# Gate tables laid by token tile, the last tile stored in four portions, and the first four u tables fetched while the gates are still being spread

## What is computed

```python
def peer_ffn(h, w_query, sub_keys, expert_u, expert_v):
    ...
    idx = jnp.take_along_axis(cand_i, pos, axis=-1).reshape(t_count, PEER_HEADS * PEER_TOPK)
    gate = jax.nn.softmax(top_s, axis=-1).reshape(t_count, PEER_HEADS * PEER_TOPK).astype(h.dtype)
    def block(args):
        tb, ib, gb = args
        act = jax.nn.gelu(jnp.einsum('pkd,pd->pk', expert_u[ib], tb), approximate=False) * gb
        return jnp.einsum('pk,pkd->pd', act, expert_v[ib])
```

## Time and profile before

| | |
|---|---|
| median of 3 runs | 4523.65 us (4521.7 to 4831.31) |
| profiled execution, own time | 4513.02 us |
| its span | 4511.1 us |
| TensorE products busy | 3640.2 us, 81% |
| VectorE, ScalarE busy | 2232.9 us (49%), 1565.4 us (35%) |
| spreading, 512 tokens | about 969 to 1155 us of the span |
| experts, 512 tokens | about 1155 to 2117 us |
| spreading, 256 tokens | about 2481 to 2592 us |
| experts, 256 tokens | about 2592 to 3070 us |

### The profile page before, as it was taken

The page is one execution under the profiler, slowest core; times in us unless marked ns, Lnnn a source line. Parts: engine busy times, 40 slices in busy tenths (PEclk is TensorE's granted clock), DMA queues, the critical chain, the costliest instruction groups (busy, mean ns, idle before and its releaser), DMA issues. The chain is left out here.

```text
span 4511.1 us, 58281 instructions
## 1 busy us (share of the span) xinstructions
PE 3640.2 (81%) x19637; PEld 2637.3 (58%) x19637; DVE 2232.9 (49%) x4378; ACT 1565.4 (35%) x2639; POOL 168.1 (4%) x344
## 2 busy tenths in 40 slices
PE   7958987958699999998885599998367767767776
PEld 5638965547588888886555589997236322222223
DVE  5535643999566666665358778884442100000001
ACT  4424432138344444442241666663122111111111
POOL 0015600000000000000000000000000000000000
PEclk8979988979899999999897899999669788788888
DMA  4320023407654444553111599993212599999996
GB/s 181 112 78 13 14 94 121 168 26 221 223 186 176 168 174 179 186 186 131 55 47 38 150 371 312 311 310 123 112 38 85 211 428 427 428 428 427 427 428 272
DMA packets 331811, 909.62 MB, mean 202 GB/s; under 512 B 46592, under 2 KB 167168, under 8 KB 306176
## 3 DMA queue, kind: packets, MB, share of 16 engines
q1 hardware_dynamic: 331648, 907.42, 53.4%
HBM read 854.38 MB, written 52.95 MB: 201 GB/s over the span
## 5 line engine op out<-in xcount | busy, mean ns | idle before, releaser
L2002 PE MATMUL pd<-h_parts,u_parts 128*128 128x512 f32 x2048 | 472.5, 391 | 38.1 <-DVE u_parts L2088 38.1
L2015 PE MATMUL po<-act_parts,v_parts 128*128 128x512 f32 x2048 | 483.5, 393 | 9.4 <-DVE v_parts L2093 2.8
L2002 PEld LDWEIGHTS pd<-h_parts,u_parts 128*128 128x128 f32 x2048 | 386.3, 189 | 119.1 <-DVE u_parts L2088 38.3
L2015 PEld LDWEIGHTS po<-act_parts,v_parts 128*128 128x128 f32 x2048 | 383.7, 189 | 104.2 <-DVE v_parts L2093 21.2
L3126 PE MATMUL pb<-moe_ring,moe_xs 128*32 128x512 f32 x2048 | 330.7, 757 | 140.0 <-DMA moe_ring<-in_moe_gu 125.1
L3177 DVE TENSOR_TENSOR moe_hidden<-moe_silu,pg 128x512 f32<-128x512 f32 x16 | 11.0, 688 | 661.6 <-PE pg L3115 576.2
L2206 PE MATMUL pd<-h_parts,u_parts 128*128 128x256 f32 x2048 | 268.1, 284 | 38.5 <-DVE u_parts L2285 38.5
L2206 PEld LDWEIGHTS pd<-h_parts,u_parts 128*128 128x128 f32 x2048 | 264.6, 192 | 50.1 <-DVE u_parts L2285 39.1
L2216 PE MATMUL po<-v_parts,act_parts 128*128 128x512 f32 x1024 | 260.0, 398 | 0.9 <-DVE act_parts L2301 0.9
L395 PE MATMUL ps<-h_terms,w_terms 128*128 128x512 f32 x960 | 224.8, 397 | 37.6 <-DVE w_terms L408 37.6
L2052 ACT ACTIVATE acts<-pd 128x512 f32<-128x512 f32 x128 | 76.5, 598 | 492.7 <-PE pd L2002 492.7
(11 more groups left out here) (486 smaller groups left out, 5839.0 us busy)
## 6 DMA issues: line engine op xcount, KB each, us to landing
moe_ring<-in_moe_gu SPq DMA_DIRECT2D x128, 2048.0 KB, 27.0
u_stream<-in_peer_u SPq DMA_DIRECT2D x256, 512.0 KB, 6.1
v_stream<-in_peer_v SPq DMA_DIRECT2D x256, 512.0 KB, 4.3
moe_ring<-in_moe_down SPq DMA_DIRECT2D x64, 2048.0 KB, 26.3
ada_ring<-in_ada_w SPq DMA_DIRECT2D x20, 2048.0 KB, 14.2
g_stream<-peer_gates SPq DMA_DIRECT2D x128, 256.0 KB, 5.5
peer_gates<-gate_stage_even SPq DMA_DIRECT2D x3, 8192.0 KB, 30.3
peer_gates<-gate_stage_odd SPq DMA_DIRECT2D x3, 8192.0 KB, 30.3
```

The lines of the kernel that those rows point to most:

```text
L2002: m = pe.matmul(pd[:, j, 0:T], us[:, j, w, c], h[:, w, c], start=(c + w == 0), stop=(c == DC - 1 and w == 1))
L2015: m = pe.matmul(po[:, (c + b) % 4, 0:T], vs[:, j, w, (c + b) * P:(c + b) * P + P], aparts[:, 4 * half + j, w], start=(j + w == 0), stop=(j ...
```

## The change

- The sets are written out one after the other instead of in loops. On VectorE is_first now stands ahead of is_second; the product with the gate follows it.
- The gate tensor in HBM is laid out [tile, i2, i1, token of the tile]. A tile's store is 64 KB in one piece for each partition. A table's g is then read as 128 partitions x 4 (wide) or 2 (narrow) pieces of 512 B.
- The last tile's store is issued as four portions (LastTile), 32 values of i1 each, 16 KB a partition. The end of the spreading stage waits for the tiles before it, not for these. Whoever needs the gates, or writes over the odd stage, waits in the experts stage for the portions concerned.
- The indicator matrices first_ind and second_ind now lie in the four slots of the ring of u tables (u_stream). When the last but one set is multiplied, SyncE fetches u tables 0 and 1 into the two slots that it used, and after the last set tables 2 and 3.
- The buffers of the experts are laid so that the odd stage lies under those which are needed late: in the wide layer v, its parts and the activation parts, in the narrow one v0 to v3 (portion 0), half of the v parts (portion 1), u4 to u7 (portion 2), v4 to v7 (portion 3).
- In the narrow layer the first eight tables are fetched in another order.

The diff, cut to its core:

```diff
-                        dve.tensor_tensor(is_second[:, x], number4, marks(1), ALU.is_equal).then_inc(second.h, 1)
...
-                        dve.tensor_tensor(is_first[:, x], number4, marks(0), ALU.is_equal).then_inc(first.h, 1)
+                    dve.tensor_tensor(is_first[:, x], number4, marks(0, t0), ALU.is_equal).then_inc(first.h, 1)
...
+                    dve.tensor_tensor(is_second[:, x], number4, marks(1, t0), ALU.is_equal).then_inc(second.h, 1)
+                    dve.wait_ge(second.h, second.at(n + 1))
...
             @block.sync
             def _(sp):
-                for tile in range(tiles):
-                    sp.wait_ge(taken.h, taken.at(4 + (tile + 1) * TURNS * 4))
-                    sp.dma_start(gates[:, :, tile * P:tile * P + P].rearrange("i p t -> p i t"), stage[tile % 2][:]).then_inc(written[tile % 2].h, DMA_DONE)
-                for w in written:
-                    sp.wait_ge(w.h, w.at(DMA_DONE * tiles // 2))
+                for tile in range(tiles - 1):
+                    sp.wait_ge(taken.h, taken.at(2 * PER * (tile + 1)))
+                    sp.dma_start(gates[tile], stage[tile % 2][:]).then_inc(written[tile % 2].h, DMA_DONE)
+                for x in range(2):
+                    sp.wait_ge(joined.h, joined.at(2 * (ALL - 1 + x)))
+                    for j in range(2 * x, 2 * x + 2):
+                        fetch_u(k, sp, tables, u, j)
+                sp.wait_ge(taken.h, taken.at(2 * ALL))
+                last.write(sp, gates, stage[(tiles - 1) % 2])
+                for tile in range(max(0, tiles - 3), tiles - 1):
+                    sp.wait_ge(written[tile % 2].h, written[tile % 2].at(DMA_DONE * (tile // 2 + 1)))
...
+class LastTile:
+    def write(self, eng, gates, stage):
+        for n in range(self.PARTS):
+            rows = slice(n * self.ROWS, (n + 1) * self.ROWS)
+            eng.dma_start(gates[self.tile, :, rows], stage[:, rows]).then_inc(self.landed[n].h, DMA_DONE)
...
 def experts_wide(k, u, v, gates, h, acc, xT, gain, us, ub, last):
...
-                    sp.dma_start(gb[:, j], gates[bass.ds(s * 4 + j, 1)].rearrange("a p t -> (a p) t")).then_inc(g_in[j].h, DMA_DONE)
+                    sp.dma_start(gb[:, j].rearrange("p (a t) -> p a t", t=P), gates[:, :, bass.ds(s * 4 + j, 1)].rearrange("a p i t -> p a (i t)")).then_inc(g_in[j].h, DMA_DONE)
...
                 for j in range(4):
-                    get_u(0, j, True)
+                    get_u(1, j, False)
+                last.wait(sp, 0)
                 for j in range(4):
                     get_g(0, j, True)
-                for j in range(4):
-                    get_u(1, j, False)
                 period(0, True)
+                last.wait(sp, 1, 2, 3)
...
                     squash(0, j, True)
                     high_u(1, j)
+                    if j == 0:
+                        last.wait(sc, 1, 2, 3)
                     high_a(0, 0, j, True)
...
 def experts_narrow(k, u, v, gates, h, xT, gain, us, spare, u0, ident, last):
...
-                for j in range(RAW):
-                    get(0, j, True)
+                last.wait(sp, 0)
+                for j in range(HALF):
+                    get_g(0, j)
+                    get_v(0, j)
+                for j in range(HALF, RAW):
+                    get_g(0, j)
+                last.wait(sp, 1, 2)
+                for j in range(HALF, RAW):
+                    get_u(0, j)
+                last.wait(sp, 3)
+                for j in range(HALF, RAW):
+                    get_v(0, j)
...
                     squash(n, j, early)
+                    if start and j == 2:
+                        last.wait(sc, 1)
                     high_v(n, j, early)
```

More of the change, by code:

```diff
@@ L1775, in peer_select, with peer_scatter @@
         x.done(2 * DMA_DONE)
-def peer_scatter(k, selT, T, consts, gates, even, terms):
+def peer_scatter(k, selT, T, consts, gates, even, odd, tables, u, terms, last):
     nc = k.nc
@@ new lines, in take @@
+                def take(n, b):
+                    tile, at = n // PER, (n % PER) * SET + 4 * b
+                    act.wait_ge(joined.h, joined.at(2 * n + b + 1))
+                    act.activation(stage[tile % 2][:, :, at:at + 4], ps[:, 2 * (n % 2) + b, :].rearrange("p (t n) -> p n t", t=4), ACT.Copy).then_inc(taken.h, 1)
+                widen(0)
+                widen(1)
+                for n in range(ALL):
+                    tile = n // PER
+                    if n % PER == 0 and tile >= 2:
+                        act.wait_ge(written[tile % 2].h, written[tile % 2].at(DMA_DONE * (tile // 2)))
+                    take(n, 0)
+                    take(n, 1)
+                    if n + 2 < ALL:
+                        widen(n + 2)
@@ new lines, with __init__, wait, done @@
+class LastTile:
+    PARTS = 4
+    ROWS = NK // PARTS
+    def __init__(self, k, tiles):
+        self.tile = tiles - 1
+        self.landed = [k.sig(f"sc_last{n}") for n in range(self.PARTS)]
+    def write(self, eng, gates, stage):
+        for n in range(self.PARTS):
+            rows = slice(n * self.ROWS, (n + 1) * self.ROWS)
+            eng.dma_start(gates[self.tile, :, rows], stage[:, rows]).then_inc(self.landed[n].h, DMA_DONE)
+    def wait(self, eng, *parts):
+        for n in parts:
+            eng.wait_ge(self.landed[n].h, self.landed[n].at(DMA_DONE))
+    def done(self):
+        for s in self.landed:
+            s.done(DMA_DONE)
@@ L1928, in done, with experts_wide @@
         self.high.done(DC)
-def experts_wide(k, u, v, gates, h, acc, xT, gain, us):
+def experts_wide(k, u, v, gates, h, acc, xT, gain, us, ub, last):
     nc = k.nc
@@ L2153, in experts_wide, with experts_narrow @@
     added.done(N_SUPER * DC)
-def experts_narrow(k, u, v, gates, h, xT, gain, us, spare, ident):
+def experts_narrow(k, u, v, gates, h, xT, gain, us, spare, u0, ident, last):
     nc = k.nc
```

186 lines of the change are left out of this document (88 added, 98 removed).

## The result

| | before | changed |
|---|---|---|
| median of 7 runs each | 4519.28 us | 4495.99 us |
| range of them | 4510.6 to 4523.65 us, and one of 4831.31 | 4489.75 to 4501.08 us |
| ratio of the runs, 95% interval | | 0.995 (0.994 to 0.9959) |
| profiled execution, its span | 4513.02, 4511.1 us | 4501.08, 4499.3 us |

The change takes 23 us, 0.5%, which is a real gain and less than the 2% that would have counted as faster. The forecast was 22.2 us. The one run of 4831.31 us was in a slower state of the chip and isn't in the ratio.

What follows compares the result with a forecast made beforehand. Two seams of some 75 us, with only a store and a fetch at work, were taken as the gain, VectorE's spreading pace and the DMA queue as risks; 11.8 + 10.4 = 22.2 us off 4523.65 gives 4502, range 4484 to 4532.

Steps and rivals of the forecast that it cites:

- Part 1: Spreading on VectorE: the product waits for the comparison just before it, costing 0.115 us a set, 11.1 us in all.
- the 0.35 us row: VectorE's idle time after the cast of the keys, behind a dependency and a branch; the high-end price per set.
- Rival 2: Spreading: VectorE's wait costs 0.43 us a set, not 0.115; 30 us more than forecast, 4532 us; chance 0.09.
- Part 2: Gates laid by tile: 8.39 MB stored in 19.7 us in place of 28.9; smaller g reads stay hidden, cost 0.
- Rival 1: Seams: the store stays at 28.9 us, both seams end 9.2 us later than forecast; 4520 us; chance 0.13.
- Rival 4: Experts: 512 B g reads at wide pitch are slow in HBM; 4672 us; chance 0.04 full, 0.04 mild.
- The pitch effect: Experts' g reads: large row pitches slow packets to about 58 ns, a narrow table 3.5 us, still hidden, sum unchanged.
- Part 3: Wide seam: early u tables start TensorE sooner, table 4 waits behind the store; net of VectorE's cost 11.8 us gained.
- The clock's 2.9 us: Wide seam: after 7 us idle TensorE loses its clock, and 2.9 us of the gain go again.
- Part 4: Narrow seam: first second-layer product at 2594.4, then u4 late at 2602.3; net gain 10.4 us.
- Rival 3: Seams: the queue doesn't hold u4 and g0 back until all portions pass; gain some 40 us, 4484; chance 0.06.

Runs made afterwards that it cites:

- e1: Changed kernel with VectorE's old order in the spreading (is_second, is_first, product); ratio to the kernel before 0.9934.
- e7: Changed kernel with the gates in the old layout (512 B store packets) and the last tile stored by one DMA; ratio to the kernel before 0.9981.
- e4: Changed kernel with the last tile stored by one DMA instead of four portions; ratio to the kernel before 0.9963.
- e2: Changed kernel with the gates laid [i1, i2, token] as before (512 B store packets), four portions kept; ratio to the kernel before 0.9984.
- e3: Changed kernel with the last tile's four portions issued by ScalarE on its own queue; ratio to the kernel before 0.9958.
- e6: Changed kernel with the wide layer's fetches issued g0, u4, g1, u5 and so on, not u4 to u7 then g0 to g3; ratio to the kernel before 0.9934.
- e9: Changed kernel with VectorE's old order and g0, u4, g1, u5 and so on, store on SyncE's queue; median 4484.54 us, ratio to the kernel before 0.9926.
- e5: Changed kernel with u0 to u3 fetched behind the last tile's portions, not ahead of them; ratio to the kernel before 0.9972.
- e8: Changed kernel with VectorE's old order, portions on ScalarE's queue, and g and u4 to u7 issued alternately; ratio to the kernel before 0.9923.

## Why the prediction was right

**Part 1, the order on VectorE.** Right, mechanism and size. Forecast 0.115 us a set and 11.1 us, measured 0.12 and 11.4 (e1). The price was taken from a plain dependent pair elsewhere in the trace (rows at 959.73 and 960.99 in the earlier trace rows) and not from the 0.35 us row behind a branch. Rival 2 is out. The statement that the loops cost nothing was slightly wrong: the rewriting saved 2.2 us. It holds for VectorE's 2.34 us a set, but not for the first set of each further tile (2.74).

**Part 2, the gates laid by tile.** Right for the new store, too large for the difference. The estimate of 422 GB/s for large store packets, drawn from two rows for small ones, stands beside 429 measured. In part that is luck: it rests on the step from 290 GB/s at 512 B to 350 at 1 KB, and e7 shows 512 B packets at 350 too. The 9.2 us by which each store should get shorter were 7.1 in the wide layer and 4.9 in the narrow one, from issue to landing with four u tables ahead (e7 against e4). Rival 1 is out, and with it the Trainium skill's figure (DMA: Bandwidth & Descriptors, Specifications) that 512 B is enough for line rate: this chip stored at 290 GB/s, for a while at 350, with 512 B, and at 429 with 16 KB. (The two layouts also differ in where in HBM the pieces go; no run varies the size alone.) What the layout is worth is shown by two pairs: 11.4 us with a single store (e7 against e4) and 12.9 with four portions (e2 against the changed kernel), about half of the change's gain and more than any other part. The reads of 512 B cost nothing, as forecast. From the wide seam's end to the narrow spreading it is 1289.0 us against 1288.2, and in the narrow experts, from table 5 to the row with the last products with v, both layouts take 463.9 us (changed 463.90, before 463.89, e2 463.89). The rise of the DMA share from 0.48 to 0.51 is just the step that the forecast's sizes give, (0.93 - 0.69) / 7.2 = 0.03. Rival 4 is out. The pitch effect of the same page (Latency and other measured facts), which by the prediction's reckoning would have doubled these packets and made the share 0.64, doesn't appear. It isn't refuted by that: the page gives it for the pitch from partition to partition, which is 64 KB here; the 8 MB lie between the pieces of one partition.

**Part 3, the wide seam.** The mechanism was right in each step: table 0 as soon as the split of h is done, a gap ahead of table 4, its cause u4 and g0 behind the store in one queue, and a cold clock after it. Table 0 came 10.8 us after the last set's products, forecast 10.9. Table 4 came 37.7 after them, forecast 35.5, and that is where the term was mis-sized by 2.1 us. I let the DMAs run at 425 GB/s from the first issue. In the profile they move 123 GB/s in the two microseconds after it (1.4 us lost) and 358 while the u tables, the store and the stage's end overlap (5 us x (1 - 358/429) = 0.8 us lost). Not all of it comes again: with the same queue e1 has table 4 at 37.1. The clock's 2.9 us came true, but with luck: tables 4 to 7 take 17.4 us against 4 x 3.64 = 14.6 here, while in e1, e3, e4 and e6 to e9 they lose 1.7 to 2.0 after a gap. And there was more idleness to lose the clock in than forecast, 9.5 us ahead of table 4 and not 7. Net gain 16.9 - 6.2 = 10.7 us, forecast 11.8.

**Part 4, the narrow seam.** The first product with v came 33.3 us after the last set, forecast 32.1, and the net gain is 14.0 - 3.0 = 11.0 us, forecast 10.4. The late one was u4 after v0, as said: TensorE waited 0.35 us for u4's split until 2597.30, 41.1 us after the last set, forecast 40.0.

**Rival 3** had the smaller chance and was wrong as well, but it deserved its test. Its condition, that the store and what follows share one queue, can be taken away (e3), and what it promised didn't come: the bound was never the order of one queue against another but the bytes ahead of g0 on engines that are full. The order within SyncE's own list (e6) brought table 4 forward by 4.4 us, a second queue by 1.0.

**The sum.** 22.2 us forecast, 23 by medians, 21.7 by the four stretches: +9.2 for VectorE's pace net of the loops, -30.9 for the seams. The small misses (a longer wait for table 4, the loops' 2.2) nearly cancel. As a time the forecast was 4502 us and the measured median is 4495.99; 4.4 of these 6 us are the kernel before, whose median was 4523.65 when the forecast was made and is 4519.28 over all seven runs. Of the seams' gain the runs price the layout (11.4 to 12.9), the early fetch (7.5) and the portions (2.7). That the stage no longer ends with the last store, where the buffers lie and the narrow layer's new order of fetching were not taken back one by one; what they are worth is argued from the timelines. Two costs that the change paid without need stood in the prediction but weren't weighed as such: the order on VectorE, which nothing required, and four u tables ahead of the g table that the first gate needs.

## What to carry to other kernels

When a queue is full, the next stage starts when the last thing that its first instruction needs has come; put that thing first, and count the bytes ahead of it, whatever queue they are on. On a vector engine that sets the pace, keep an instruction without a dependency between a producer and its consumer, and price the dependency from a plain pair in the trace. Lay out an intermediate tensor for the transfer that nothing hides, here the store in large pieces, and let the hidden one, here the read, take the small pieces.

## What the runs showed of the hardware that I had not expected

- **Issuing a DMA can take as long as moving it.** Four stores of 4096 packets of 512 B held SyncE for 22.14 us (e2). One store of 16384 such packets was issued in 0.43 us, but the four loads behind it stood for 23.89 us (e7). Even with large packets the second g table waited behind a full queue, 11.31 us in its issue (of 17.07 for all four, changed kernel). So the queue has room for a limited amount of outstanding work; how much, and in what unit, these runs don't settle. A branch or barrier behind such an issue is reached late, although no wait stands in the code. In these seams that cost nothing, as the store bounds them (e2 and e7 are equally long).
- **The portions alone gained nothing in the wide seam and 4.9 us in the narrow one** (e4). With small packets they put table 0 off, to 27.9 us after the last set from 10.8 with one store (e2, e7), and the seams stayed as long.
- **A second queue doesn't bring the last byte sooner.** It brought one transfer 5.7 us forward and the last needed one 1.1, of which e1 shows half without a second queue (e3).
- **A later start can cost less than it seems**, since the second gap and its cold start go away: in e5 table 0 was 17.6 us later and the seam 4.7 us longer.
- **The time lost at 1.2 GHz after a gap doesn't follow the gap's length.** The four tables behind it lost 1.7 us after 3.35 us of idleness (e8), 1.7 after 15.47 (e7) and 2.9 after 9.52 (changed).
